# A two-layer hybrid encoder: the mixer's work laid out in forty slots, one for each weight unit

## What is computed

```python
h = rms_norm(x, mix_norm_g[l]); proj = h @ w_in[l]          # 1024 -> 4096: eight parts of 512
y_a = diff_attention(da_q, da_k, da_v, ...)                 # 4 heads, rotary, two softmaxes per head
#   weights = softmax(q1 k1) - lam * softmax(q2 k2); o = rms_norm(weights @ v) * (1 - lam_init)
y_b = hgrn2_bidirectional(hg_q, hg_zf, hg_zb, hg_i, hg_g, lb_f, lb_b)   # 4 heads, gated recurrence both ways
#   log f from sigmoid(z) and a lower bound, key = (1 - lb) * sigmoid(-z); o = rms_norm(o) * silu(g)
x = x + concat(y_a, y_b) @ w_out[l]                         # 1024 -> 1024
u = rms_norm(x, ffn_norm_g[l]) @ w_up[l]                    # 1024 -> 5632, then a convolution of width 3
x = x + (silu(a) * v) @ w_down[l]                           # 2816 -> 1024
```

## Time and profile before

| | us |
|---|---|
| three runs | 1524.94, 1528.08, 1529.03 (median 1528.08) |
| the profiled execution | 1527.44 |
| its span, first to last instruction | 1525.6 |
| mean granted clock of PE | 0.988 |

### The profile page before, as it was taken

How to read it: one execution, slowest core, us unless ns; L and a number is a source line. 1 busy time by engine, 2 the same in 40 slices (tenths; PEclk the granted TensorE clock), 3 DMA queues, 4 the chain that set the end, 5 groups by cost and what they waited for, 6 DMA issues and landing times.

```text
span 1525.6 us, 19057 instructions
## 1 busy us (share of the span) xinstructions
PE 1440.0 (94%) x6476; PEld 1131.9 (74%) x6476; DVE 874.6 (57%) x1104; ACT 605.2 (40%) x864; POOL 784.7 (51%) x620
## 2 busy tenths in 40 slices
PE   6999998869899999999999999979798999999999
PEld 5777676637678888888878776765486788888887
DVE  7886566491576767610168774674906767777001
ACT  6333434552444444421342434336425444444111
POOL 4777465344634444444577773652446444443443
PEclk9999999999999999999999999999899999999999
DMA  4322111001222223223222221110022222222223
GB/s 158 97 69 70 55 54 44 28 1 56 71 95 90 102 83 105 87 98 105 95 85 95 70 68 44 56 42 28 1 72 81 85 94 96 96 96 96 97 96 111
DMA packets 33894, 117.21 MB, mean 77 GB/s; under 512 B 3888, under 2 KB 4272, under 8 KB 33840
## 3 DMA queue, kind: packets, MB, share of 16 engines
q1 hardware_dynamic: 33408, 115.69, 22.2%
q10 hardware_dynamic: 432, 0.80, 0.2%
HBM read 114.38 MB, written 2.10 MB: 76 GB/s over the span
## 4 chain that ended last, share of the span: by engine, by line
PE 75%; DVE 9%; issue 8%; POOL 5%; ACT 1%; DMA 0%; SPq 0%; POOLq 0%; DVEq 0%; ACTq 0%
PE bank L491 22%; PE bank L493 21%; PE bank L492 21%; PE bank L586 3%; POOL wL L468 2%; PE bank L556 2%; DVE E L1217 2%; POOL rstd L351 2%; POOL wL L402 2%; DVE QQ L1195 1%; DVE sm L1209 1%; DVE W L1220 1%; PE bank L531 1%; PE bank L532 1%; PE bank L624 1%
## 5 line engine op out<-in xcount | busy, mean ns | idle before, releaser
L491 PE MATMUL bank<-hH,wH 128*128 128x512 f32 x1344 | 539.8, 402 | 23.4 <-DVE hL L339 16.6
L468 POOL TENSOR_TENSOR wL<-raw,wH 128x1024 fp32r<-128x1024 f32 x136 | 326.9, 2404 | 410.4 <-ACT wH L796 359.2
L493 PE MATMUL bank<-hL,wH 128*128 128x512 f32 x1344 | 526.9, 392 | 0.0
L492 PE MATMUL bank<-hH,wL 128*128 128x512 f32 x1344 | 526.6, 392 | 0.0
L402 POOL TENSOR_TENSOR wL<-raw,wH 128x256 fp32r<-128x256 f32 x300 | 276.2, 951 | 208.7 <-ACT wH L788 208.7
L491 PEld LDWEIGHTS bank<-hH,wH 128*128 128x128 f32 x1344 | 254.5, 189 | 94.7 <-issue 27.4
L493 PEld LDWEIGHTS bank<-hL,wH 128*128 128x128 f32 x1344 | 254.2, 189 | 54.8
L492 PEld LDWEIGHTS bank<-hH,wL 128*128 128x128 f32 x1344 | 254.7, 189 | 50.6 <-issue 1.4
L796 ACT ACTIVATE wH<-raw 128x1024 fp32r<-128x1024 f32 x116 | 122.6, 1057 | 184.1 <-PE bank L493 181.3
L788 ACT ACTIVATE wH<-raw 128x1024 fp32r<-128x1024 f32 x95 | 100.2, 1055 | 234.5 <-PE bank L493 233.9
L491 PE MATMUL bank<-gH,wH 128*128 (+1 forms) x352 | 137.3, 390 | 0.0
(11 more groups left out here) (155 smaller groups left out, 1607.7 us busy)
## 6 DMA issues: line engine op xcount, KB each, us to landing
raw<-wts SPq DMA_DIRECT2D x211, 512.0 KB, 3.2
x<-xT SPq DMA_DIRECT2D x8, 256.0 KB, 6.2
outT<-x SPq DMA_DIRECT2D x8, 256.0 KB, 2.0
raw<-wts ACTq DMA_DIRECT2D x1, 512.0 KB, 4.8
QK<-pos SPq DMA_DIRECT2D x2, 256.0 KB, 5.3
C<-cst ACTq DMA_DIRECT2D x1, 259.5 KB, 6.2
R<-par SPq DMA_DIRECT2D x2, 108.0 KB, 2.6
M<-msk SPq DMA_DIRECT2D x1, 112.0 KB, 6.9
```

Source lines behind the costliest of these rows:

```text
L468: pool.tensor_tensor(wL[:, s, :], raw[:, s, :], wH[:, s, :].bitcast(F32), ALU.subtract)\
L491: pe.matmul(out, wH[:, s, a:a + P], rhs_h, start=first, stop=False)
L492: pe.matmul(out, wL[:, s, a:a + P], rhs_h, start=False, stop=False)
L493: return pe.matmul(out, wH[:, s, a:a + P], rhs_l, start=False, stop=last)
```

## The change

`schedule()` is replaced by forty slots, one for each unit of `w_in` and `w_out` (`ORDER`). In a slot PE does, in this order: one item, the scores of one step, a transposition to tokens, the first half of the unit, the `turn` of the step before, the second half, a mean of squares, the `values` of the step before. Items stand in slots 7 to 30, steps in slots 17 to 32, so every step has a unit beside it. POOL does `split` of the next unit and then grows the keys; its squares and output halves are gone to ACT (`stat_square`, `high_out`) and DVE (`low_out`), into new tiles `yH`, `yL`. The units are in a new order, with the first pair's gates and queries first, and `dk`, `dq`, `dv` of a head together.

```diff
-    order = [("unit", u) for u in range(U_HQ + 2)]
...
+ORDER = [("zf", 0), ("zf", 1), ("zb", 0), ("zb", 1), ("hq", 0), ("hq", 1),
...
+FIRST_ITEM, FIRST_STEP = 7, 17
...
+STATS = {13: ("dk", 0), 14: ("dq", 0), 18: ("dk", 1), 19: ("dq", 1), 20: ("hgo", 0), 21: ("dk", 2), 22: ("dq", 2),
...
-                    for kind, n in ORDER:
...
+                    for s in range(SLOTS):
+                        if item_of(s) is not None:
+                            item(item_of(s))
+                        if step_of(s) is not None:
+                            scores(step_of(s))
+                        if tokens_of(s) is not None:
+                            to_tokens(tokens_of(s))
+                        half = unit_half if s < N_IN else out_half
+                        half(s, 0)
+                        if s == LATE:
+                            stat(STATS[s])
+                        if step_of(s - 1) is not None:
+                            turn(step_of(s - 1))
+                        half(s, 1)
+                        if s in STATS and s != LATE:
+                            stat(STATS[s])
+                        if step_of(s - 1) is not None:
+                            values(step_of(s - 1))
```

```diff
-                        pe.matmul(bank[7][:], rotg[:, n // 4, :], QK[:, n, :], start=True, stop=True).then_inc(qk_aux.sem, 1)
...
+                        sp_.dma_start(swp[p:p + HD // 2, n % 2, :], tile[q:q + HD // 2, at, :]).then_inc(swapped[n % 2].sem, 16)
...
+                        if l and 0 < s <= N_IN and ORDER[s - 1] in GATES:
+                            forget(GATES.index(ORDER[s - 1]))
```

More of the change, by code:

```diff
@@ L49 @@
 STEPS = 16
-HEAD_ORDER = [("hg", 0), ("hg", 1), ("da", 0), ("da", 1), ("hg", 2), ("hg", 3), ("da", 2), ("da", 3)]
-AHEAD = 8
-def schedule():
-    order = [("unit", u) for u in range(U_HQ + 2)]
[L56 to L77, removed]
@@ L403, in split, with split_whole, splits @@
                         m.then_inc(w_split.sem, 1)
-                    def split_now(u):
-                        if u < UNITS:
-                            split(u, u % 2)
+                    def split_whole(u, s, step=None):
+                        pool.wait_ge(*w_high.at(l, u + 1, step))
+                        pool.tensor_tensor(wL[:, s, :], raw[:, s, :], wH[:, s, :].bitcast(F32), ALU.subtract)\
+                            .then_inc(w_split.sem, 1)
+                    def splits(first, end):
+                        with pool.Fori(first // 2, end // 2) as j:
+                            for s in range(2):
+                                split_whole(s, s, j * 2)
                     def grow(pair, lv):
@@ L464, in splits @@
[L464 to L476 removed]
+                    if l == 0:
+                        split_whole(0, 0)
+                        split_whole(1, 1)
@@ new lines, in _ @@
+                    for s in range(SLOTS):
+                        n = item_of(s)
+                        if s:
+                            split(s + 1)
+                        if n is not None and 1 <= n % (LEVELS + 1) <= 8:
+                            grow(*divmod(n, LEVELS + 1))
+                        if s >= N_IN + 4:
+                            for k in ((1, 2, 3), (4,), (5,), (6,))[s - N_IN - 4]:
+                                add_square(pool, l, k, 1)
+                    split_whole(U_UP + 1, 1)
@@ L977, in _, with silus, norm_tile @@
+                    def silus(first, end):
+                        for hd in range(first, end):
+                            act.wait_ge(*unit_ev.at(l, AT[("hg", hd)] + 1))
+                            act.activation(gs(hd), gs(hd), ACT.Silu).then_inc(gs_done.sem, 1)
+                        logs()
+                    def norm_tile(k):
                         act.wait_ge(*x_upd.at(l, k + 1))
-                        if k == KT - 1:
-                            act.wait_ge(*w_used.at(l, U_UP))
```

999 lines of the change are left out of this document (483 added, 516 removed), and 4 rows, old and new, of the table ORDER.

## The result

The changed kernel takes 1460.03 us (four runs, 1459.84 to 1460.28) against 1527.2 us for the kernel before (four runs): a ratio of 0.9561, 95% interval 0.9544 to 0.9577, so 67 us less. The profiled execution took 1460.28 us with a span of 1458.7, 67.2 us under the profiled 1527.44 of before. 61.7 us had been forecast, 1466 us as a median. So the direction and the range were right, the sum is 5.5 us too cautious, and behind that small number stand one large error to one side and two to the other.

The account below looks back on a forecast made before the run. PE was taken to bound the kernel, busy 1440.0 of 1525.6 us. Gains of 23.6 (layer 0), 26.3 (layer 1) and 11.8 us (FFN's start) made 61.7, so 1466 us; own range 1452 to 1480, with rivals 1436 to 1500.

Parts of the forecast that it names:

- What PE must do: Both mixers: time left when PE only works; 342.3 us in layer 0, 338.6 us in layer 1.
- (1): Slots 8 to 12, without means: PE's part takes 7.3 us, the ring 8.95; 8 us a layer lost.
- The ring: Between items: ACT's rounding, POOL's split, totals and growing, ACT's copy of `kx`, then the next rounding; 8.95 us without steps.
- (2): Slots 20 to 26, with steps: PE and the ring both take 10.9 us; allowance 3 us a layer.
- (3): Start: layer 0's first mean 2.7 us later; old waits kept, 2 us in layer 0, 1 in layer 1.
- (4): Slots 31 and 32: silus and four table loads on ACT's queue, which PE's values wait for; 2 us a layer.
- (5): Slots 36 to 39: three `add_square` stand on POOL before the next split; 1.5 us a layer.
- The FFN's start: Third FFN column comes sooner, seven of eight x tiles being ready; 5.7 + 6.1 = 11.8 us gained.
- Rival 1: Mixer slots: POOL and DVE slow each other, the ring sets the pace; 21 to 52 us lost, middle 1500; chance 0.20.
- Rival 2: Mixers: everything hidden under PE; (1), (2), (4), (5) and the start's 2.7 us gone; 1434 us; chance 0.13.
- Rival 3: Attention steps: all 32 turns still wait 2.7 us for `W`; 86 us, 1552, slower than before; chance 0.04.
- Rival 4: Weight loads come late behind the swap's wait for an eviction, idle time only moves; 1528 us; chance 0.03.

## Why the prediction was right, and where it wasn't

**What PE must do** was reckoned at 342.3 and 338.6 us (idle time, rotations and clock taken out of the earlier trace rows); its busy time is 341.3 and 339.2. That step held to 1 us, and the run with the useless matmuls shows that the rotations' 0.86 us were all on the path. But the nearness is in part luck. Each measured time holds one fall of the clock (1.7 us) and some 1.2 us of the slower pitch in the output projection; at the forecast's own terms it is 338.4 and 336.3, so 3.9 and 2.3 us too much was entered. A part of that is the clock, read from two digits: 0.01 and 0.02 made 3.9 and 7.6 us, and the stretches at 1.2 GHz in the trace before (10.2 and 17.1 us) make 5.1 and 8.5. The rest stays open.

**What PE waits in the mixers**: the terms make 19.2 and 15.5 us, 34.7; measured are 11.1 and 10.8 (352.40 - 341.32 and 350.00 - 339.24), 21.9. By terms, from the wait list:

**(1) The ring in slots 8 to 12**, 16 us in both layers: the waits before the items are 7.6 + 5.6 = 13.2, and two falls of the clock between them (85 and 805 us) take 3.4 of the same stretch. Without these falls, in the run with the bounds first, the waits alone are 16.7. Right in place, mechanism and size, and the run with POOL's order reversed confirms it.

**(2) The slots with steps**, 6 us for two things that are equal: no item waits there, and a mean waits 0.2 us in each layer. This is the step that failed. The lengths were right, 10.9 us of ring beside 10.9 us of PE (measured rounds: 11.2, 10.4 and 9.9), and so was the order, with the exponentials ahead of the rounding. What I left out is the lead: the ring enters these slots with `kx` 6.8 us early, uneven rounds take from that, and it never goes under 2.4. A loss of 0.5 to 1 us a slot would have needed a ring without reserve.

**(3) The start and what I kept of its waits**, 5.7 us: 0.6 for the mean, 0.8 and 1.5 for the units behind it and 0.4 for `hL`, 3.3. ACT's squares begin at 17.90, reckoned 17.9, but unit 1 itself is late, so little of it shows. What was missed stands before that: the first matmul at 12.59 and not at 10.17, since the bounds' transfer stands behind the first unit's and DVE's copy met POOL's split. At unit 3 only 1.0 us of the 2.4 is left (34.0 against 33.0), and the run with the bounds first wins nothing. The mean of the first layer comes at 24.98, 1.9 us later than before, where 2.7 had been reckoned.

**(4) Silus and table loads**, 4 us: 1.1, at a turn that waits for `rstd`. **(5) The additions**, 3 us: 1.7 in each layer at the second output unit after them, 3.4.

So the mixers gained 63.4 us and not 49.9; 12.8 of these 13.5 are waits that were entered and didn't come, most of all (2) and (4).

**The FFN's start**: 5.7 + 6.1 forecast; the third column comes 11.4 us after the first in both layers, 5.9 and 6.2 less than before.

**What no step had**: 6.5 us in the down projections by the slower pitch, and some 2.5 in the output projections (384 matmuls over yH and yL with the same 6.6 ns). "The rest of the matmuls are the same in number and size" was true, and didn't make them equally long.

The account in full, by the starts of units: 63.4 + 12.1 - 2.4 - 6.2 = 66.9 us of span, where 6.2 is what the two layers lose behind the third FFN column. So the forecast missed by 5 us with errors of 13.5 to one side and 8.6 to the other; that they stand against each other is luck. The range is also not what its own terms make: their low ends give 1447 and their high ends 1483, taken for each layer, and not 1452 and 1480.

**The rivals.** Rival 1 (POOL and DVE slow each other and set the pace) didn't happen at its size, but its mechanism is shown: 10.1 us for longer pieces. The longest rounds of the ring, 11.0 and 10.0 us before the items at 83.84 and 803.52, have splits of 4.17 and 3.63 us with DVE at work on SBUF beside them, against 3.26 in the round shown; that this is the reason is argued, not tested by itself. Nor was the forecast's 3.27 us free of such company: DVE's growing, with two SBUF inputs, ran beside it from 112.36 on. Rival 2 (all hidden) was right for terms (2) and (4), wrong for the ring. Rival 3 (turns wait for `W`) is refuted also in its weaker form, without the half unit. Rival 4: no wait for a load of weights is in PE's list, and ACT's rounding waits for one once, 2.5 us at the start.

## What to carry to other kernels

When serial work with its waits is laid beside units of a stream, count the busy time of the bounding engine first: it gave the mixer to 1 us, though partly by luck. The allowances for "equal" queues were the error: ask how far ahead the other queue starts. Then look for rings over the other engines: on an engine that does both, the work that feeds the next step (growing) goes ahead of the work that is needed a slot later (the split), if its ring is longer than the slot.

Two engines that exclude each other want short instructions, even where long ones are cheaper: 45 us less work on POOL in one mixer, and the kernel 10 us longer. And a wait of PE can cost more than its length, by a fall of the clock behind it, but only where PE sets the pace: 1.6 us at 395 and at 1115 us, nothing at 805. Since falls come and go between runs with the same waits, compare two versions stretch by stretch before a difference of a few us is given to an edit.

## What the hardware showed that I had not expected

The same 128x512 matmuls at a full clock, with nothing waiting, came every 226.7 or every 233.3 ns, by program and, as far as two profiles of one kernel tell, not by execution, and 88 bytes less of an unused tile moved a kernel from one to the other (6.4 us). It is worth counting matmuls in a full stretch before and after a change in the layout of SBUF.

A DVE copy of 128x8 took 2.25 us beside a GpSimd subtraction, and 0.17 alone. Tiny instructions at the head of a queue can be the dearest ones there.
